# Weight sums of the down projection's sets: another order and other buffers

## The chip, the core and the metric

The kernel runs on one core of a Trainium2 chip. TensorE does the matrix products, VectorE (DVE) and ScalarE (ACT) the elementwise work, GpSimd (POOL) small things, and SyncE (SP) issues most transfers. The metric is the time of one execution on the device in microseconds. Lower is better.

## The reference

The function is two transformer blocks in a row over 256 tokens of width 2048, in float32: a gated-linear-attention mixer and an MLP with a squared ReLU, then a hybrid mixer, a cross attention and a convolutional feed-forward. What matters here is the MLP of the first block, which is

```
def _sq_relu_mlp(h, w_up, w_down):
    a = jax.nn.relu(h @ w_up)          # 2048 -> 8192
    return (a * a) @ w_down            # 8192 -> 2048
```

with a normalised input and its result added to h.

## The kernel before

All weights arrive as a stream of chunks of 128 x 2048 float32 (1 MB). A product in float32 precision is made of three: each operand is split into a high part and a low part, and TensorE adds high x high, high x low and low x high. ScalarE makes the high part of each chunk (`split`, L1198), VectorE subtracts it from the chunk and so makes the low part (`split`, L1874), in place over the raw chunk. The raw chunks go through a ring of four slots, and the high parts through four of their own. A chunk that is used for all 256 tokens takes 24 matmuls of 512 columns (`chunk`, L615 to L617), one that is used for a half of them takes 12 (`product`, L757 to L759).

The MLP works in four parts of 2048 hidden units. A part has up to 38 items, numbered 0 to 37 here: items 0 to 7 are plain up chunks, 8 to 18 a set (`up_pair`), 19 to 26 plain down chunks for the output blocks 0 and 1, and 27 to 37 again a set (`down_pair`), in the first three parts. A set computes blocks 2 and 3 of the output from sums of operands, in the manner of Strassen's algorithm with fewer products: with B11, B12, B21 and B22 for four weight chunks it needs B11+B12, B12+B22, B11+B12+B22 and that plus B21. VectorE forms these in `sums_of_weights`. For the down set the sums are t1, t3, t2 and t4 and stand as items 31, 35, 32 and 36 in TensorE's order; item 29 is B22 itself ("d22"), item 27 is B11 and item 33 is B21. B12 and B22 are fetched aside, right behind the ring's transfer for item 21, and the sum with B12 is then written over it. VectorE also forms sums of the activations, u_raw (`sums_of_a`, c=21 and 22), of which ScalarE makes u_hi and VectorE u_lo (L2147); item 29 is the first that needs them.

Order is fixed by the program. VectorE and ScalarE each run one loop over c = 0 to 37 in a part, and each takes its instructions strictly in that order. In iteration c VectorE does, one after another: `pair_to_h`, `sums_of_weights`, activation work, the add of a finished block to h (blocks 0 and 1 at c=25 and 26, L1950), the subtraction for item c+3, and last `sums_of_a`. ScalarE does u_hi at c=23 ahead of its copy for item 26. TensorE waits for the count `lo_ready` before each item, which the subtraction for that item raises; for item 28 it also waits for block 0's add to h, and for item 29 for u_lo and block 1's. ScalarE's copy for item i waits for the end of item i-4 on TensorE, and for a sum it waits for `sum_ready` to reach the position that the tuple `SUMS` gives. SyncE refills a ring slot when the item that used it is done.

Addresses: a_s is the start of a 48 KB region. The first 8 KB hold `turned` and the next 8 KB `sq` during the squares of the activations, so that a sum may be written over them only when `sq_moved` and `a_low` say that they are done. The 8 KB at a_s + 16 K receive B12.

Of the kernel before, what the change touches and what calls it, by code (L numbers as in the profile page):

```python
# [17 lines left out]
def build(nc, x, x_turned, mem, mem_turned, stream, cols, rows, wglow, wab, wgu, shapes, masks, out):  # L18
# [15 lines left out]
    ACT, ALU, AX = mybir.ActivationFunctionType, mybir.AluOpType, mybir.AxisListType  # L34
# [5 lines left out]
    GROUPS, GROUP = 4, 38  # L40
# [7 lines left out]
    with ExitStack() as ctx:  # L48
# [15 lines left out]
        K = 1024  # L64
# [31 lines left out]
        a_s = take(48 * K)  # L96
# [40 lines left out]
        a_sum = {"T1": a_a + 8 * K, "T3": a_a + 24 * K, "T2": a_s + 16 * K, "T4": a_s + 24 * K}  # L137
        a_sum["b22"] = a_sum["T4"]
        sum_raw = {t: sb(f"raw_{t}", [P, CH], F32, a) for t, a in a_sum.items()}
        sum_lo = {t: sb(f"lo_{t}", [P, CH], F32R, a) for t, a in a_sum.items()}  # L140
        s_raw = sb("s_raw", [P, 4, 4, P], F32, a_s + 32 * K)
        s_lo = sb("s_lo", [P, 4, 4, P], F32R, a_s + 32 * K)
        a_sum.update({"t3": a_s, "t2": a_s + 8 * K, "t1": a_s + 16 * K, "t4": a_s + 24 * K, "d22": a_s + 24 * K})
        for t in ("t1", "t2", "t3", "t4", "d22"):
            sum_raw[t] = sb(f"raw_{t}", [P, CH], F32, a_sum[t])
            sum_lo[t] = sb(f"lo_{t}", [P, CH], F32R, a_sum[t])
# [125 lines left out]
        sum_ready, b12_in, b22_in = sem("sum_ready"), sem("b12_in"), sem("b22_in")  # L272
# [7 lines left out]
        nat_turned, sq_moved, a_high, a_low = [sem(n) for n in ("nat_turned", "sq_moved", "a_high", "a_low")]  # L280
# [76 lines left out]
        def landing(c):  # L357
            return 16 * (c // SLOTS + 1)
# [67 lines left out]
        C_GLA, C_OUT, C_MLP, C_2 = 0, 48, 64, 64 + sum(LENGTH)  # L426
# [1 line left out]
        assert C_FFN + 96 == NITEM  # L428

        SUM_AT = {10: "b22", 12: "T1", 13: "T2", 15: "T3", 16: "T4"}  # L430
        SUMS = (("T1", "T3", "T2", "T4"), ("t3", "t1", "t2", "t4"))
        DOWN_SUM_AT = {29: "d22", 31: "t1", 32: "t2", 35: "t3", 36: "t4"}
        DOWN_AT = {27: (0, 2), 28: (2, 2), 30: (3, 2), 33: (1, 2), 34: (2, 3), 37: (3, 3)}
        UP_AT = {8: (0, 2), 9: (2, 2), 11: (3, 2), 14: (1, 2), 17: (2, 3), 18: (3, 3)}
# [16 lines left out]
        def down_chunk(g, q, b):  # L451
            return C_MLP + 32 * g + 16 + 4 * b + q
# [30 lines left out]
        @block.sync  # L483
        def _(sp):
            x_rows = x.rearrange("(m p) n -> p m n", p=P)

            def quarter_of_x(n):
                sp.dma_start(h[:, :, n * N:(n + 1) * N], x_rows[:, :, n * N:(n + 1) * N]).then_inc(x_in, 16)

            def turned_x(k0, k1, done):  # L490
                sp.dma_start(x_raw[:, k0:k1], x_turned[:, k0:k1]).then_inc(done, 16)

            def weights(c, k):
                sp.dma_start(w_raw[:, c, k * N:(k + 1) * N], stream[c][:, k * N:(k + 1) * N]).then_inc(w_part[c][k], 16)

            turned_x(0, 2, xT_in[0])
            weights(0, 0)
            weights(0, 1)
            turned_x(2, 4, xT_in[NB])
            weights(0, 2)  # L500
            weights(0, 3)
            for c in range(1, EARLY):
                turned_x(4 * c, 4 * c + 4, xT_in[c])
                for k in range(4):
                    weights(c, k)
            sp.dma_start(ident, shapes[:, 0:P]).then_inc(cst_in, 16)
            sp.dma_start(mask01[:], shapes[:, 2 * P:2 * P + SEQ]).then_inc(mask_in, 16)
            for n in range(SLOTS, len(RING)):
                c = RING[n]
                sp.wait_ge(used, RING[n - SLOTS] + 1)  # L510
                sp.dma_start(w_raw[:, n % SLOTS], stream[source(c)]).then_inc(landed[n % SLOTS], 16)
                if C_MLP <= c < C_2 and (c - C_MLP) % GROUP == 3:
                    sp.dma_start(sum_raw["T3"][:], stream[up_chunk((c - C_MLP) // GROUP, 0, 3)]).then_inc(b12_in, 16)
                    sp.dma_start(sum_raw["b22"][:], stream[up_chunk((c - C_MLP) // GROUP, 1, 3)]).then_inc(b22_in, 16)
                if C_MLP <= c < C_MLP + 3 * GROUP and (c - C_MLP) % GROUP == 21:
                    sp.dma_start(sum_raw["t1"][:], stream[down_chunk((c - C_MLP) // GROUP, 0, 3)]).then_inc(b12_in, 16)
                    sp.dma_start(sum_raw["d22"][:], stream[down_chunk((c - C_MLP) // GROUP, 1, 3)]).then_inc(b22_in, 16)
                if c == SLOTS + 1:
                    for n in range(NB):
                        quarter_of_x(n)  # L520
                if c == SLOTS + 4:
                    sp.dma_start(ones, shapes[:, P:2 * P]).then_inc(cst_in, 16)
            for m in range(M):
                sp.wait_ge(fin_dve, 3 * m + 1)
                sp.dma_start(out[m * P:(m + 1) * P, 2 * N:3 * N], h[:, m, 2 * N:3 * N]).then_inc(out_done, 16)
                sp.wait_ge(fin_dve, 3 * m + 3)
                sp.dma_start(out[m * P:(m + 1) * P, 3 * N:4 * N], hlast[:, m]).then_inc(out_done, 16)
            sp.wait_ge(out_done, 16 * 2 * NB)
# [1332 lines left out]
        def _(dve):  # L1861
# [229 lines left out]
            def sums_of_weights(part, c):  # L2091

                first = C_MLP + GROUP * part

                def weights_in(k):
                    dve.wait_ge(landed[PLACE[first + k] % SLOTS], landing(PLACE[first + k]))
                    return raw(first + k)

                if c == 5:
                    b11 = weights_in(8)  # L2100
                    dve.wait_ge(b12_in, 32 * part + 16)
                    dve.tensor_tensor(sum_raw["T1"][:], b11, sum_raw["T3"][:], ALU.add).then_inc(sum_ready, 1)
                if c == 6:
                    dve.wait_ge(b22_in, 32 * part + 16)
                    dve.tensor_tensor(sum_raw["T3"][:], sum_raw["T3"][:], sum_raw["b22"][:], ALU.add).then_inc(sum_ready, 1)
                    dve.wait_ge(sum_ready, 8 * part + 1)
                    dve.tensor_tensor(sum_raw["T2"][:], sum_raw["T1"][:], sum_raw["b22"][:], ALU.add).then_inc(sum_ready, 1)
                if c == 10:
                    b21 = weights_in(14)
                    dve.wait_ge(used, first + 11)  # L2110
                    dve.wait_ge(sum_ready, 8 * part + 3)
                    dve.tensor_tensor(sum_raw["T4"][:], sum_raw["T2"][:], b21, ALU.add).then_inc(sum_ready, 1)
                if part == 3:
                    return
                if c == 23:
                    dve.wait_ge(b12_in, 32 * part + 32)
                    dve.wait_ge(b22_in, 32 * part + 32)
                    dve.wait_ge(sq_moved, 4 * part + 4)
                    dve.tensor_tensor(sum_raw["t3"][:], sum_raw["t1"][:], sum_raw["d22"][:], ALU.add).then_inc(sum_ready, 1)
                if c == 24:  # L2120
                    b11 = weights_in(27)
                    dve.wait_ge(sum_ready, 8 * part + 5)
                    dve.tensor_tensor(sum_raw["t1"][:], sum_raw["t1"][:], b11, ALU.add).then_inc(sum_ready, 1)
                    dve.wait_ge(a_low, 4 * part + 4)
                    dve.tensor_tensor(sum_raw["t2"][:], sum_raw["t3"][:], b11, ALU.add).then_inc(sum_ready, 1)
                if c == 29:
                    b21 = weights_in(33)
                    dve.wait_ge(used, first + 30)
                    dve.wait_ge(sum_ready, 8 * part + 7)
                    dve.tensor_tensor(sum_raw["t4"][:], sum_raw["t2"][:], b21, ALU.add).then_inc(sum_ready, 1)  # L2130

            def sums_of_a(part, c):

                rows_ = [[v_sum[:, q, :, m * P:(m + 1) * P] for q in range(2)] for m in range(M)]
                if c == 21:
                    dve.wait_ge(nat_turned, 4 * part + 4)
                    for q in range(2):
                        ins = dve.tensor_tensor(v_sum[:, q], a_hi[:, 4 * q:4 * q + 4].bitcast(F32), a_lo[:, 4 * q:4 * q + 4].bitcast(F32), ALU.add)
                    link(ins)
                if c == 22:  # L2140
                    dve.tensor_tensor(u_raw[:, 2], rows_[0][0], rows_[1][0], ALU.subtract)
                    link(dve.tensor_tensor(u_raw[:, 0], rows_[1][0], rows_[1][1], ALU.subtract))
                    link(dve.tensor_tensor(u_raw[:, 1], u_raw[:, 0], rows_[0][0], ALU.subtract))
                    dve.tensor_tensor(u_raw[:, 3], u_raw[:, 1], rows_[0][1], ALU.add).then_inc(s_formed, 1)
                if c == 25:
                    dve.wait_ge(pair_out, pair_step(part, "s"))
                    dve.tensor_tensor(u_lo[:], u_raw[:], u_hi[:].bitcast(F32), ALU.subtract).then_inc(s_formed, 1)  # L2147

# [401 lines left out]
            for nb in range(NB):  # L2550
                for j in range(16):
                    c = 50 + 16 * nb + j
# [306 lines left out]
```

## Time and profile before

| | us |
|---|---|
| median of 3 runs | 2473.53 (2472.73 to 2474.16) |
| profiled execution | 2473.63 |
| its span, first to last instruction | 2471.8 |
| TensorE matmuls busy | 2459.8 (100%) |
| VectorE busy | 1660.3 (67%) |
| ScalarE busy | 1608.6 (65%) |

The duration of a matmul in the profile runs past the start of the next one, so "busy" is not the same as "at its peak"; the distance between two starts tells more. The rows used below are from three views. A wait row says who waited for whom, then the total, the number of times and the longest, in us. A timeline row has the start in us from the span's start, the duration, engine, line, operation, tiles and how many instructions were merged, and in brackets the idle time of the engine before it and what ended that. A window row has, for a stretch, the busy time and number of instructions of each engine, the granted TensorE clock (1.00 is 2.4 GHz, 0.50 is 1.2 GHz), the DMA share and the rate in GB/s. Lines are those of the kernel before as the profile numbers them.

### The profile page before, as it was taken

What the parts mean: (1) busy time and instruction counts of PE and PEld (TensorE: products, weight loads), DVE (VectorE), ACT (ScalarE), POOL (GpSimd) and SP (SyncE); (2) the same over time, 40 slices, a digit from 0 to 9 for tenths busy, and PEclk for the clock granted to TensorE, in tenths of its full rate; (3) what the DMA queues carried; (4) which work ended last, traced back from release to release, by engine and by line L of the source; (5) the groups of instructions that cost most, each with busy time, mean ns of one, the idle gap of its engine ahead of it and who ended that gap; (6) DMA issues with size and microseconds to landing.
All of it is one profiled execution on the core that took longest, in us unless ns stands there. A gap on an engine that the chain in (4) does not pass through costs nothing.

```text
span 2471.8 us, 29802 instructions
## 1 busy us (share of the span) xinstructions
PE 2459.8 (100%) x12367; PEld 2030.9 (82%) x12367; DVE 1660.3 (67%) x1371; ACT 1608.6 (65%) x2119; POOL 33.4 (1%) x41
## 2 busy tenths in 40 slices
PE   9999999999999999999999999999999999999998
PEld 7887788888888888888888888888888888888887
DVE  5865658787778868577764785545666677646675
ACT  6545778856748658776465684545586788638873
POOL 0000000000000000000000000000000000000000
PEclk9999999999999999999999999999999999999999
DMA  8554556545554555545443445555655555555554
GB/s 289 187 190 168 173 188 237 190 181 208 206 203 178 215 207 188 189 171 198 158 149 140 157 174 195 196 188 197 261 189 176 192 194 188 199 191 190 200 189 153
DMA packets 69366, 472.36 MB, mean 191 GB/s; under 512 B 7912, under 2 KB 8352, under 8 KB 13424
## 3 DMA queue, kind: packets, MB, share of 16 engines
q1 hardware_dynamic: 67040, 460.62, 51.5%
q0 software_dynamic: 1312, 7.73, 0.8%
q8 instruction: 97, 1.59, 0.3%
q10 hardware_dynamic: 880, 2.11, 0.2%
q14 instruction: 37, 0.30, 0.0%
HBM read 468.33 MB, written 2.11 MB: 190 GB/s over the span
## 4 chain that ended last, share of the span: by engine, by line
PE 93%; DVE 2%; ACT 2%; issue 1%; DMA 1%; SPq 0%; POOLq 0%; POOL 0%; DVEq 0%; ACTq 0%
PE acc L615 28%; PE acc L617 28%; PE acc L616 28%; DMA w_raw<-in_stream 1%; PE tp L759 1%; PE tp L758 1%; PE tp L757 1%; ACT w_hi L1198 1%; DVE w_lo L1874 1%; PE acc L757 1%; PE acc L759 1%; PE acc L758 1%; ACT sq L1391 1%; PE tp L979 1%; PE tp L912 0%
## 5 line engine op out<-in xcount | busy, mean ns | idle before, releaser
L1874 DVE TENSOR_TENSOR w_lo<-w_raw,w_hi 128x2048 fp32r<-128x2048 f32 x416 | 950.9, 2288 | 616.4 <-ACT w_hi L1198 614.2
L1198 ACT ACTIVATE w_hi<-w_raw 128x2048 fp32r<-128x2048 f32 x416 | 795.6, 1915 | 394.3 <-DMA w_raw<-in_stream 346.8
L615 PE MATMUL acc<-w_hi,x_hi 128*128 128x512 f32 (+1 forms) x2112 | 826.2, 391 | 1.4 <-DVE w_lo L1881 0.6
L617 PE MATMUL acc<-w_hi,x_lo 128*128 128x512 f32 (+1 forms) x2112 | 819.7, 388 | 0.0
L616 PE MATMUL acc<-w_lo,x_hi 128*128 128x512 f32 (+1 forms) x2112 | 819.5, 388 | 0.0
L615 PEld LDWEIGHTS acc<-w_hi,x_hi 128*128 128x128 f32 x2112 | 396.8, 188 | 86.8 <-issue 2.9
L617 PEld LDWEIGHTS acc<-w_hi,x_lo 128*128 128x128 f32 x2112 | 396.7, 188 | 81.3
L616 PEld LDWEIGHTS acc<-w_lo,x_hi 128*128 128x128 f32 x2112 | 396.9, 188 | 80.3 <-issue 1.0
L615 PE MATMUL acc<-w_hi,a_hi 128*128 128x512 f32 x1024 | 400.0, 391 | 0.4 <-DVE w_lo L1874 0.2
L616 PE MATMUL acc<-w_lo,a_hi 128*128 128x512 f32 x1024 | 399.0, 390 | 0.0
L617 PE MATMUL acc<-w_hi,a_lo 128*128 128x512 f32 x1024 | 398.9, 390 | 0.0
L615 PEld LDWEIGHTS acc<-w_hi,a_hi 128*128 128x128 f32 x1024 | 192.3, 188 | 42.4 <-DVE w_lo L1874 1.6
L617 PEld LDWEIGHTS acc<-w_hi,a_lo 128*128 128x128 f32 x1024 | 192.3, 188 | 39.7
L616 PEld LDWEIGHTS acc<-w_lo,a_hi 128*128 128x128 f32 x1024 | 192.3, 188 | 39.5
L1391 ACT ACTIVATE sq<-turned 32x256 f32<-32x256 f32 x256 | 106.2, 415 | 6.9 <-DVE turned L2204 3.4
L1788 ACT ACTIVATE fm<-fturned 32x256 f32<-32x256 f32 x256 | 106.2, 415 | 4.5 <-DVE fturned L2689 1.5
L1215 ACT ACTIVATE nat<-acc,rstd 128x512 f32<-128x512 f32 (+1 forms) x80 | 50.0, 677 | 76.4 <-PE acc L617 75.2
L1215 ACT ACTIVATE nat<-acc,rhalf 128x512 f32<-128x512 f32 x36 | 22.8, 684 | 66.8 <-PE acc L617 66.7
L1950 DVE TENSOR_TENSOR h<-acc,h 128x1024 f32<-128x1024 f32 x35 | 42.7, 1221 | 27.4 <-PE acc L617 27.4
L1237 ACT ACTIVATE sq<-turned 32x256 f32<-32x256 f32 x112 | 46.5, 415 | 9.4 <-DVE turned L1917 8.1
L615 PE MATMUL acc<-w_hi,m_hi 128*128 128x512 f32 x128 | 49.9, 390 | 0.0
L616 PE MATMUL acc<-w_lo,m_hi 128*128 128x512 f32 x128 | 49.9, 389 | 0.0
(482 smaller groups left out, 1954.2 us busy)
## 6 DMA issues: line engine op xcount, KB each, us to landing
w_raw<-in_stream SPq DMA_DIRECT2D x416, 1024.0 KB, 4.8
w_raw<-in_stream SPq DMA_DIRECT2D x16, 256.0 KB, 8.2
raw_T<-in_stream SPq DMA_DIRECT2D x4, 1024.0 KB, 7.2
raw_b<-in_stream SPq DMA_DIRECT2D x4, 1024.0 KB, 8.9
raw_t<-in_stream SPq DMA_DIRECT2D x3, 1024.0 KB, 7.0
raw_d<-in_stream SPq DMA_DIRECT2D x3, 1024.0 KB, 10.2
h<-in_x SPq DMA_DIRECT2D x4, 512.0 KB, 14.0
frow<-in_rows POOLq DMA_DIRECT2D x2, 1024.0 KB, 6.5
```

What stands on the lines that cost most here:

```text
L615: pe.matmul(dst, xh, wh[:, k], start=first and k == 0, stop=False)
L616: pe.matmul(dst, xh, wl[:, k], start=False, stop=False)
L617: mm = pe.matmul(dst, xl, wh[:, k], start=False, stop=last and k == n_k - 1)
L757: pe.matmul(dst, xh[:, k], wh[:, k], start=start and k == 0, stop=False, skip_group_check=not start)
L758: pe.matmul(dst, xh[:, k], wl[:, k], start=False, stop=False, skip_group_check=not start)
L759: mm = pe.matmul(dst, xl[:, k], wh[:, k], start=False, stop=stop and k == 3, skip_group_check=not start)
L1198: act.activation(w_hi[:, c % SLOTS], raw(c), ACT.Copy).then_inc(hi_ready, 1)
L1215: ins = act.activation(dst[:, m], src[:, m], func, scale=scales[:, j, m:m + 1])
L1237: ins = act.activation(dst[32 * to:32 * to + 32, :, :, q], src[32 * q:32 * q + 32, :, :, to], ACT.Copy, scale=scale)
L1391: ins = act.activation(dst[32 * to:32 * to + 32, :, :, q], src[32 * q:32 * q + 32, :, :, to], ACT.Square)
L1788: ins = act.activation(dst[32 * to:32 * to + 32, :, :, q], src[32 * q:32 * q + 32, :, :, to], ACT.Copy)
L1874: dve.tensor_tensor(low_part(c), raw(c), w_hi[:, c % SLOTS].bitcast(F32), ALU.subtract).then_inc(lo_ready, 1)
```

## The change

The four sums of a down set are formed in the order t1, t3, t2, t4, and not t3, t1, t2, t4. B12 is fetched into the buffer t3, which has the address that t1 had, so it lands in the same place; t1 has the address that t3 had. t1 = B11 + B12 stays at c=24, now as the first sum. t3 = B12 + B22 goes from c=23 to c=25, in place over B12. t2 goes from c=24 to c=26 and is computed as t1 + B22, not as t3 + B11. The subtraction u_lo goes from c=25 to c=24. The waits go with the sums. TensorE's program is the same.

```
-        a_sum.update({"t3": a_s, "t2": a_s + 8 * K, "t1": a_s + 16 * K, "t4": a_s + 24 * K, "d22": a_s + 24 * K})
+        a_sum.update({"t1": a_s, "t2": a_s + 8 * K, "t3": a_s + 16 * K, "t4": a_s + 24 * K, "d22": a_s + 24 * K})
...
-        SUMS = (("T1", "T3", "T2", "T4"), ("t3", "t1", "t2", "t4"))
+        SUMS = (("T1", "T3", "T2", "T4"), ("t1", "t3", "t2", "t4"))
...
-                    sp.dma_start(sum_raw["t1"][:], stream[down_chunk((c - C_MLP) // GROUP, 0, 3)]).then_inc(b12_in, 16)
+                    sp.dma_start(sum_raw["t3"][:], stream[down_chunk((c - C_MLP) // GROUP, 0, 3)]).then_inc(b12_in, 16)
...
-                if c == 23:
-                    dve.wait_ge(b12_in, 32 * part + 32)
-                    dve.wait_ge(b22_in, 32 * part + 32)
-                    dve.wait_ge(sq_moved, 4 * part + 4)
-                    dve.tensor_tensor(sum_raw["t3"][:], sum_raw["t1"][:], sum_raw["d22"][:], ALU.add).then_inc(sum_ready, 1)
                 if c == 24:
                     b11 = weights_in(27)
+                    dve.wait_ge(b12_in, 32 * part + 32)
+                    dve.wait_ge(sq_moved, 4 * part + 4)
+                    dve.tensor_tensor(sum_raw["t1"][:], b11, sum_raw["t3"][:], ALU.add).then_inc(sum_ready, 1)
+                if c == 25:
+                    dve.wait_ge(b22_in, 32 * part + 32)
+                    dve.tensor_tensor(sum_raw["t3"][:], sum_raw["t3"][:], sum_raw["d22"][:], ALU.add).then_inc(sum_ready, 1)
+                if c == 26:
+                    dve.wait_ge(a_low, 4 * part + 4)
                     dve.wait_ge(sum_ready, 8 * part + 5)
-                    dve.tensor_tensor(sum_raw["t1"][:], sum_raw["t1"][:], b11, ALU.add).then_inc(sum_ready, 1)
-                    dve.wait_ge(a_low, 4 * part + 4)
-                    dve.tensor_tensor(sum_raw["t2"][:], sum_raw["t3"][:], b11, ALU.add).then_inc(sum_ready, 1)
+                    dve.tensor_tensor(sum_raw["t2"][:], sum_raw["t1"][:], sum_raw["d22"][:], ALU.add).then_inc(sum_ready, 1)
...
-                if c == 25:
+                if c == 24:
                     dve.wait_ge(pair_out, pair_step(part, "s"))
                     dve.tensor_tensor(u_lo[:], u_raw[:], u_hi[:].bitcast(F32), ALU.subtract).then_inc(s_formed, 1)
```

## Rows read from the trace of the kernel before

**Rows 1.** The page's head and its first part: busy us, share, instructions.
```profile
span 2471.8 us, 29802 instructions
...
PE 2459.8 (100%) x12367; PEld 2030.9 (82%) x12367; DVE 1660.3 (67%) x1371; ACT 1608.6 (65%) x2119; POOL 33.4 (1%) x41
```

**Rows 2.** The list of waits, TensorE: total us, times, longest.
```profile
PE acc L615 <- DVE w_lo L1874: 0.5, 2, 0.3
```

**Rows 3.** Timeline of TensorE, first part: first matmuls of items 27, 28, 29, 32.
```profile
508.62 0.39 PE L757 MATMUL tp<-w_hi,a_hi 128*128 128x512 f32 x1
...
511.12 0.39 PE L759 MATMUL tp<-w_hi,a_lo 128*128 128x512 f32 x1
511.62 0.50 PE L615 MATMUL acc<-w_hi,a_hi 128*128 128x512 f32 x1
...
517.25 0.47 PE L757 MATMUL acc<-w_hi,u_hi 128*128 128x512 f32 x1
...
528.23 0.39 PE L757 MATMUL tp<-w_hi,u_hi 128*128 128x512 f32 x1
```

**Rows 4.** Timeline of VectorE, first part.
```profile
495.47 2.29 DVE L2119 TENSOR_TENSOR raw_t<-raw_t,raw_d 128x2048 f32<-128x2048 f32 x1
499.34 2.29 DVE L1874 TENSOR_TENSOR w_lo<-w_raw,w_hi 128x2048 fp32r<-128x2048 f32 x1 [1.58 <-ACT w_hi L1198]
501.55 2.28 DVE L2123 TENSOR_TENSOR raw_t<-raw_t,w_raw 128x2048 f32<-128x2048 f32 x1
...
505.95 2.28 DVE L1874 TENSOR_TENSOR w_lo<-w_raw,w_hi 128x2048 fp32r<-128x2048 f32 x1
...
509.29 2.28 DVE L1874 TENSOR_TENSOR w_lo<-w_raw,w_hi 128x2048 fp32r<-128x2048 f32 x1
511.49 2.28 DVE L2147 TENSOR_TENSOR u_lo<-u_raw,u_hi 128x2048 fp32r<-128x2048 f32 x1
...
514.82 2.28 DVE L1874 TENSOR_TENSOR lo_d<-raw_d,w_hi 128x2048 fp32r<-128x2048 f32 x1
...
524.22 2.29 DVE L1874 TENSOR_TENSOR lo_t<-raw_t,w_hi 128x2048 fp32r<-128x2048 f32 x1
...
541.32 2.29 DVE L1874 TENSOR_TENSOR w_lo<-w_raw,w_hi 128x2048 fp32r<-128x2048 f32 x1 [1.94 <-ACT w_hi L1198]
```

**Rows 5.** Timelines of VectorE and TensorE, item 28 of second and third part.
```profile
678.41 2.28 DVE L1874 TENSOR_TENSOR w_lo<-w_raw,w_hi 128x2048 fp32r<-128x2048 f32 x1
...
680.74 0.50 PE L615 MATMUL acc<-w_hi,a_hi 128*128 128x512 f32 x1
...
847.72 2.28 DVE L1874 TENSOR_TENSOR w_lo<-w_raw,w_hi 128x2048 fp32r<-128x2048 f32 x1
...
850.05 0.51 PE L615 MATMUL acc<-w_hi,a_hi 128*128 128x512 f32 x1 [0.18 <-DVE w_lo L1874]
```

**Rows 6.** Timeline of ScalarE, first part: u_hi and the copies of 26 and 27.
```profile
495.58 1.92 ACT L1451 ACTIVATE u_hi<-u_raw 128x2048 fp32r<-128x2048 f32 x1 [5.01 <-DVE u_raw L2144]
497.41 3.70 ACT L1198 ACTIVATE w_hi<-w_raw 128x2048 fp32r<-128x2048 f32 x2
```

**Rows 7.** Timeline of TensorE, a longer gap near the kernel's start.
```profile
13.45 0.50 PE L615 MATMUL acc<-w_hi,x_hi 128*128 128x512 f32 x1 [0.64 <-DVE w_lo L1881]
13.78 0.39 PE L616 MATMUL acc<-w_lo,x_hi 128*128 128x512 f32 x1
```

**Rows 8.** TensorE's last matmul, and windows behind it (PEclk is third from the end).
```profile
2463.55 0.39 PE L617 MATMUL acc<-w_hi,a_lo 128*128 128x512 f32 x1
...
2465.00:2466.00 1.00, 0.00 (x0) 0.00 (x0) 0.56 (x2) 0.43 (x2) 0.30 (x1) 1.00 0.00 0
2466.00:2467.00 1.00, 0.00 (x0) 0.00 (x0) 0.71 (x2) 0.65 (x1) 0.25 (x1) 0.73 0.00 0
```

**Rows 9.** Timeline of TensorE's weight loads, the kernel's first matmuls.
```profile
1.59 0.15 PEld L728 LDWEIGHTS acc<-junk 128*128 128x128 bf16 x1 [0.28 <-issue]
...
5.43 0.33 PEld L728 LDWEIGHTS acc<-junk 128*128 128x128 bf16 x2 [0.28 <-issue]
```

## The prediction

> **What bounds the kernel now.** The page's first part comes first: TensorE is busy for 2459.8 of 2471.8 us [rows 1]. Whatever the change does to VectorE counts only where it moves a matmul. The list of waits then names few for TensorE; the one that belongs to a subtraction of a weight chunk (L1874) sums to 0.5 us [rows 2]. That list understates it, because the end of a matmul is modelled: one start every 0.227 us (508.62 to 511.12 is 11 intervals) but 0.39 us of duration, so a short stall is covered by the record before it. So I read starts in the timeline. Around the start of chunk 28 of the first part two starts are 0.50 us apart, 511.12 and 511.62 [rows 3], 0.27 more than the steady interval. From 511.12 to 528.23 there are 73 intervals (24 of chunk 28, 12 of 29, 24 of 30, 12 of 31, and one), 16.6 us at 0.227; they took 17.11. About 0.55 us are lost there per part.
>
> What releases chunk 28 is seen on VectorE. Its subtraction for chunk 28 runs 509.29 to 511.57 and TensorE starts 0.05 later [rows 3, 4]. The other two parts show the same pair: subtraction 678.41 to 680.69, matmul 680.74; subtraction 847.72 to 850.00, matmul 850.05 [rows 5]. Three out of three times the end of this one subtraction sets the start of chunk 28, and TensorE has no slack there.
>
> VectorE is late because it works without a pause from 499.34 (subtraction for 26) until the 1.94 us before 541.32; no row between those two has idle time in its brackets [rows 4]. Before 499.34 it has a hole of another sort: the subtraction for 26 waits 1.58 us for ScalarE's copy of 26, which stands behind the copy u_hi (495.58), so it can't be done before 499.3 [rows 6]. VectorE reaches that point at 495.47, and the first sum of the set (L2119) lies wholly in this gap: 495.47 to 497.76 [rows 4]. It costs nothing now.
>
> **The change part by part.** Per part with a down set (three of four) VectorE has the same four sums and the same u_lo; no instruction is added or removed, and none changes its length. What counts is the order between the subtraction for 26 and that for 28.
>
> *Before:* sub 26, t1, t2, sub 27, add to h, sub 28; then u_lo, add to h, sub 29, sub 30.
> *After:* sub 26, t1, sub 27, u_lo, t3, add to h, sub 28; then t2, add to h, sub 29, sub 30.
>
> The end of c=23 loses the sum L2119: the gap before 499.34 grows from 1.58 to about 3.9 us, and nothing is gained, since the subtraction for 26 is released by ScalarE, whose two copies don't depend on the sum [rows 4, 6]. Removed: 0.
>
> c=24: t1 stays in place. t2 goes (a 2048-element operation; start to start 2.20 us, as 499.34 to 501.55 and 509.29 to 511.49 show [rows 4]). So the subtraction for 27 starts at 503.75 and not at 505.95. It ended at 508.24, with chunk 27 starting at 508.62 [rows 3, 4]: TensorE didn't wait for it, so 2.20 us earlier is worth 0. Then u_lo, 2.20, takes the place that is freed. Its input u_hi is done by 497.5 [rows 6], so it doesn't wait.
>
> c=25: the sum t3, another 2.20 us, now stands ahead of the add to h and of the subtraction for 28. Its transfers came with item 21, long before; the sums of before took the same two buffers at 495.47 without a wait [rows 4]. Nothing lets VectorE do it while idle.
>
> Sum for the subtraction for 28: −t2 + u_lo + t3 = −2.20 + 2.20 + 2.20 = +2.20 us. It starts at 511.49, ends at 513.77, and chunk 28 starts at about 513.82 in place of 511.62. Queued behind t3 on VectorE are the add to h of block 0 and subtraction 28, and TensorE waits for the second. The bounds on a 2048-element operation are 2.20 (start to start) and 2.28 to 2.29 (its full duration, if nothing overlaps). I take 2.20, since all rows in an unbroken run show it.
>
> Chunk 29: before, u_lo, the add and the subtraction for 29 followed (subtraction start 509.29 to 514.82 is 5.53 us). After, t2 is where u_lo was, equally long: again 5.53. Chunk 29 therefore keeps its present small delay, and u_lo, which it also needs, is earlier. Its subtraction starts at 517.02. Of the later ones, the subtraction for 32 starts at 524.22 and chunk 32's products at 528.23, 1.7 us after it ends [rows 3, 4]. Both sides move by 2.20, and so does ScalarE, which waits for the counts of finished chunks. t2 is ready at 515.97, ahead of ScalarE's copy of it, which waits for the end of chunk 28 at about 519.3. The fourth sum L2130 reads t2, and waits for chunk 29 as before. The 1.94 us of idle before 541.32 belongs to a wait for ScalarE that itself follows TensorE, so it pays nothing back: work follows matmuls there, and every matmul is late by 2.20.
>
> A larger stall could also have a larger ramp behind it. After 511.62 the intervals are a little long (0.34, then 0.24), part of the 0.55. At the start of the kernel a longer gap, with 0.64 us of recorded idle, ends at 13.45, and the next start follows 0.33 later [rows 7]; the ramp doesn't grow with the gap. I add 0, bound +0.15 per part. From below: the existing 0.55 per part could vanish if the order mattered in a way that I don't see, 1.65 in all.
>
> DMA: the transfer of the fourth chunk has another name, but t3 now has the address that t1 had, and its place on SP's queue stays. Cost 0. The waits on counts a_low, sum_ready and sq_moved are for events that VectorE has itself passed, or that lie before 495. Cost 0.
>
> Sum: 3 × 2.20 = 6.6 us on the profiled execution's 2473.63, which is its span 2471.8 and 1.8 around it: 2480.2. The median shown is 2473.53, 0.1 lower, so this is +0.27%.
>
> The Trainium skill ("VectorE: DVE Perf Modes", section "The DRAIN you can't avoid") has the next VectorE operation start only when the pipeline is empty. The rows of an unbroken run show a start 0.08 us ahead of the recorded end of the one before. By the rule's word an extra operation would be 2.28 and the sum 6.8 us, 2480.4; the rows decide for 2.20.
>
> **The rivals.** *The clock falls in the longer gap.* In the changed kernel TensorE would have no matmul from 511.51 to 513.82, 2.3 us, three times. At the end of the kernel the last matmul ends at 2463.94, the granted clock is 1.00 to 2466 and averages 0.73 over the next microsecond: with the two levels 2.4 and 1.2 GHz it fell at about 2466.5, after 2.5 us without a matmul [rows 8]. That is near. Against it: the gap here is shorter and has dense matmuls on both sides. What a fall would cost: in the kernel's first matmuls the loads are 0.43 us apart from 1.59 to 5.43 [rows 9], nearly twice 0.227; some 4.2 us at that pace lose 2.0 us. One to three falls give 2482.2 to 2486.2.
> The Trainium skill ("TensorE: Matmul & The Clock Gate", section "Why this matters for your kernels") warns of gaps between bursts, since idle time brings the clock down, but allows longer ones than 2.3 us; by it the sum is left at 2480.2. The row at the end of the kernel shows a fall after less idle time than it allows, so I keep the rival.
>
> *Not slower.* The wider hole at c=23 pays the operation back. With the sum gone from beside ScalarE's copies, the copy of 26 would end sooner, VectorE would begin its unbroken run earlier, and the extra operation would be done before it is missed. It decides from a subtraction for 26 that starts 2.2 us earlier, near 497.1; then nothing changes, 2473.6, and if it starts another 0.5 earlier the present loss goes too: 2472.0. For it: VectorE is ready at 495.5, so only ScalarE holds the start. Against: the copy of 26 starts at 497.41, since u_hi before it starts only at 495.58, released by u_raw, which the change doesn't touch [rows 6]; and the two copies take 3.70 us together with the sum running beside only the first moments of them.
>
> *A second wait of the same size.* One operation more is late at chunk 29 or 32 too, because a copy or sum that I count as covered isn't. One more 2.20 per part gives 2486.8. Against it: the 5.53 us that stays and the 1.7 us of slack at 32.
>
> **How the numbers follow.** Forecast 0.76, own range 2479.0 to 2481.5; clock 0.10; not slower 0.08; second wait 0.06. The range 2477.6 to 2484.0 leaves out the not-slower case, the second wait and half of the clock's, 0.19. Told apart from no change is 0.2%, 4.9 us, so slower begins at 2478.5: forecast, clock and second wait less 0.04 for a forecast that comes out small, 0.88. Within: 0.08 less 0.01, and those 0.04: 0.11. Faster 0.01, since all that can be won in this stretch is 1.65 us.
>
> **What would show it.** In the timeline of the changed kernel: a hole of 3.9 us on VectorE before the subtraction for 26; the order after it as above; subtraction 28 ending 14.4 us after the start of subtraction 26 (12.2 now); gaps of 2.7 us between matmul starts at chunk 28, three of them; the waits list with some 2.3 us each for TensorE on L1874; chunk 29 with the small delay of now; the clock 1.00 throughout. The forecast is wrong if chunk 28 starts before subtraction 28 ends, if the subtraction for 26 starts earlier than now relative to chunk 26, or if matmul intervals near 0.43 us follow the gap.

## The result and the profile after

The changed kernel takes 2482.12 us (median of 6 runs, 2481.78 to 2484.38), the kernel before 2473.79 (6 runs): ratio 1.0036, interval 1.0025 to 1.0048. It is slower by 8.3 us. The profiled execution took 2484.38, the longest of the six, with a span of 2482.6. One execution of a later kernel (the one with matmuls in the gap) took 4771.94 us at a mean granted clock of 0.512 and stands in no ratio here.

The head of the page of the changed kernel and its wait of TensorE on L1874, which answer to [rows 1, 2]:

```profile
span 2482.6 us, 29802 instructions
...
PE 2462.9 (99%) x12367; PEld 2032.3 (82%) x12367; DVE 1660.5 (67%) x1371; ACT 1609.0 (65%) x2119; POOL 33.5 (1%) x41
```
```profile
PE acc L615 <- DVE w_lo L1874: 7.9, 4, 2.7
```

The number of instructions and VectorE's and ScalarE's busy time are as before. What changed is waiting: TensorE's wait for this subtraction, 0.5 us in all, became 7.9. VectorE's timeline of the changed kernel, first part, answers to [rows 4] and to the hole of [rows 6]:

```profile
499.83 2.29 DVE L1874 TENSOR_TENSOR w_lo<-w_raw,w_hi 128x2048 fp32r<-128x2048 f32 x1 [3.79 <-ACT w_hi L1198]
502.04 2.28 DVE L2119 TENSOR_TENSOR raw_t<-w_raw,raw_t 128x2048 f32<-128x2048 f32 x1
504.25 2.28 DVE L1874 TENSOR_TENSOR w_lo<-w_raw,w_hi 128x2048 fp32r<-128x2048 f32 x1
506.45 2.28 DVE L2148 TENSOR_TENSOR u_lo<-u_raw,u_hi 128x2048 fp32r<-128x2048 f32 x1
508.65 2.28 DVE L2122 TENSOR_TENSOR raw_t<-raw_t,raw_d 128x2048 f32<-128x2048 f32 x1
510.85 1.21 DVE L1950 TENSOR_TENSOR h<-acc,h 128x1024 f32<-128x1024 f32 x1
511.99 2.28 DVE L1874 TENSOR_TENSOR w_lo<-w_raw,w_hi 128x2048 fp32r<-128x2048 f32 x1
```

The hole before the subtraction for 26 is 3.79 us where it was 1.58, and from the start of that subtraction to the end of the one for 28 it is 14.44 us (511.99 + 2.28 − 499.83) where it was 12.23. The extra 2.2 are t3 (L2122). TensorE in the same stretch, and further down its gaps in parts two and three, answer to [rows 3, 5]:

```profile
511.31 0.39 PE L759 MATMUL tp<-w_hi,a_lo 128*128 128x512 f32 x1
514.32 0.50 PE L615 MATMUL acc<-w_hi,a_hi 128*128 128x512 f32 x1 [2.62 <-DVE w_lo L1874]
514.66 0.55 PE L616 MATMUL acc<-w_lo,a_hi 128*128 128x512 f32 x1
515.01 0.63 PE L617 MATMUL acc<-w_hi,a_lo 128*128 128x512 f32 x1
515.43 0.63 PE L615 MATMUL acc<-w_hi,a_hi 128*128 128x512 f32 x1
515.86 0.63 PE L616 MATMUL acc<-w_lo,a_hi 128*128 128x512 f32 x1
...
518.30 0.39 PE L616 MATMUL acc<-w_lo,a_hi 128*128 128x512 f32 x1
518.53 0.39 PE L617 MATMUL acc<-w_hi,a_lo 128*128 128x512 f32 x1
...
687.54 0.50 PE L615 MATMUL acc<-w_hi,a_hi 128*128 128x512 f32 x1 [2.68 <-DVE w_lo L1874]
...
860.48 0.50 PE L615 MATMUL acc<-w_hi,a_hi 128*128 128x512 f32 x1 [2.35 <-DVE w_lo L1874]
```

Two things are to be seen. Item 28 starts 0.05 us after its subtraction ends, as before, and 3.01 us after the start of the last matmul of item 27. And the matmuls behind the gap start 0.43 us apart from 515.01 to 518, then 0.23 again. Windows of the changed kernel (the granted clock stands third from the end):

```profile
511.30:514.30 3.00, 0.40 (x2) 0.00 (x0) 3.00 (x3) 1.91 (x1) 0.00 (x0) 1.00 0.98 391
514.30:514.90 0.60, 0.58 (x2) 0.54 (x3) 0.60 (x1) 0.00 (x0) 0.00 (x0) 0.87 1.00 423
515.00:518.20 3.20, 3.20 (x9) 2.51 (x8) 3.20 (x3) 0.00 (x0) 0.00 (x0) 0.51 0.25 102
518.30:520.00 1.70, 1.70 (x9) 1.39 (x8) 1.70 (x2) 0.00 (x0) 0.00 (x0) 1.00 0.00 0
...
688.60:689.00 0.40, 0.40 (x3) 0.35 (x2) 0.40 (x1) 0.00 (x0) 0.00 (x0) 0.77 0.97 389
...
860.50:866.00 5.50, 5.50 (x24) 4.40 (x24) 5.50 (x4) 0.00 (x0) 0.00 (x0) 1.00 0.32 137
```

The clock, 2.4 GHz through the gap, went to 1.2 GHz shortly after it (0.87 is the mean of the first 0.6 us), when matmuls ran again, and came back at about 518.3. It did the same in the second part, where it fell at about 688.8 (the row that starts at 688.60), and not in the third (the last row).

The account of the profiled execution, +10.75 us: the gaps between matmul starts at item 28 were 0.50, 0.42 and 0.56 and are 3.01, 3.06 and 2.74, 7.3 more. From the start of item 28 to that of item 30 TensorE took 8.45, 8.47 and 8.45 us before and takes 9.90, 9.95 and 8.44 now: 1.45 and 1.48 more in the two parts with a fall and 0 in the third, 2.9 in all. The other 0.5 us lie outside what was changed: 0.2 were there before the first of these gaps (the last matmul of item 27 starts at 511.31, not 511.12), and 0.35 came in behind item 30 of the third part (from 858.50 to the last matmul at 2463.55 before, from 868.92 to 2474.32 now). Their cause is open.

### The profile page after: what moved, and what is told of

Its sections match the earlier page's. It is cut to its first block, busy times and chain, and to the rows that moved or that the text cites. A ratio compares the mean times of both kernels' runs of the same rounds, so it can differ in the third digit from the quotient of the medians.

```text
span 2482.6 us, 29802 instructions
## 1 busy us (share of the span) xinstructions
PE 2462.9 (99%) x12367; PEld 2032.3 (82%) x12367; DVE 1660.5 (67%) x1371; ACT 1609.0 (65%) x2119; POOL 33.5 (1%) x41
## 4 chain that ended last, share of the span: by engine, by line
PE 91%; DVE 3%; ACT 2%; issue 2%; DMA 1%; SPq 0%; POOLq 0%; POOL 0%; DVEq 0%; ACTq 0%
PE acc L615 28%; PE acc L617 27%; PE acc L616 27%; DMA w_raw<-in_stream 1%; ACT w_hi L1198 1%; DVE w_lo L1874 1%; PE tp L759 1%; PE tp L758 1%; PE tp L757 1%; PE acc L757 1%; PE acc L758 1%; PE acc L759 1%; ACT sq L1391 1%; PE tp L979 1%; PE tp L912 0%
## 5 line engine op out<-in xcount | busy, mean ns | idle before, releaser
L1874 DVE TENSOR_TENSOR w_lo<-w_raw,w_hi 128x2048 fp32r<-128x2048 f32 x416 | 950.8, 2288 | 625.4 <-ACT w_hi L1198 622.8
L617 PE MATMUL acc<-w_hi,m_lo 128*128 128x512 f32 x128 | 49.8, 389 | 0.0
```

The lines of the kernel that those rows point to most:

```text
L617: mm = pe.matmul(dst, xl, wh[:, k], start=False, stop=last and k == n_k - 1)
L1874: dve.tensor_tensor(low_part(c), raw(c), w_hi[:, c % SLOTS].bitcast(F32), ALU.subtract).then_inc(lo_ready, 1)
```

## The experiments

Three theories went in. A: one more operation in VectorE's unbroken run is the cost, 2.2 us a part, and the clock's falls follow from the gap. B: the new buffers, the in-place sum or the later t2 cost something themselves. C: only the late t3 matters, wherever u_lo stands. The 1.7 us that B has to explain are what the measured 8.3 has beyond the forecast's 6.6. Each kernel was run 5 to 11 times beside the kernel before, whose median was 2473.31 for the first four and 2473.88 for the rest.

**u_lo back at c=25.**

```
-                if c == 24:
+                if c == 25:
                     dve.wait_ge(pair_out, pair_step(part, "s"))
```

> The changed kernel with u_lo back at c=25, behind the subtraction for 28; the sums stay in their new order and buffers. Theory A (what counts is how many operations stand between the subtraction for 26 and that for 28, and the clock falls in the gap that one more of them makes): the count is that of the kernel before again, so no long gap, clock 0.999, 2473.8 within 0.7 us. Rival B (new buffers, in-place sum or later t2 cost something of their own, the 1.7 us beyond 6.6): 2475.5. Rival C (u_lo's place is of no account, the late sum t3 is what costs): 2482.

Measured: 2481.59 us, ratio 1.0033 (1.0021 to 1.0046). A's number, 2473.8, was wrong. The trace shows where its counting stopped too early. TensorE of this kernel:

```profile
516.69 0.39 PE L617 MATMUL acc<-w_hi,a_lo 128*128 128x512 f32 x1
519.16 0.47 PE L757 MATMUL acc<-w_hi,u_hi 128*128 128x512 f32 x1 [2.09 <-DVE lo_d L1874]
```

Up to the subtraction for 28 the count is indeed that of before. But between those for 28 and 29 now stand both u_lo and t2, where before only u_lo stood. The gap moved to item 29: 2.47, 2.50 and 2.44 us in the three parts, with one fall of the clock in the profile, behind the first, where the stretch from the start of item 29 to that of item 31 took 9.88 us against 8.25 and 8.28 in the other two. An operation that has left the hole is in the run somewhere; where u_lo stands decides only which item pays. This run alone speaks for C, whose 2482 it nearly is, and A stands only in this wider form. For the total the wider A and C then say the same, but for one point: whether it must be t3 that is late. The next run answers that.

**One more operation in the kernel before.**

```
...
-                    dve.tensor_tensor(sum_raw["t2"][:], sum_raw["t3"][:], b11, ALU.add).then_inc(sum_ready, 1)
+                    dve.tensor_tensor(sum_raw["t2"][:], sum_raw["t3"][:], b11, ALU.add).then_inc(formed_once, 1)
+                if c == 25:
+                    dve.wait_ge(sum_ready, 8 * part + 6)
+                    dve.wait_ge(formed_once, 1 * part + 1)
+                    dve.tensor_tensor(sum_raw["t2"][:, :2048], sum_raw["t1"][:, :2048], sum_raw["d22"][:, :2048], ALU.add).then_inc(sum_ready, 1)
```

> The kernel before with one more VectorE operation of 2048 elements ahead of the subtraction for 28: t2 is formed a second time at c=25. Order and buffers of the sums are those of before. A: one operation is 2.2 us in each of three parts, 6.6, and one to three falls of the clock at 1.6 us each, so 2482 to 2485, like the changed kernel. B: 2480.4, since nothing but the operation is added and the rest came with the buffers. C: 2480 to 2482 as well.

Measured: 2482.13 us, ratio 1.0035 (1.0023 to 1.0047), the changed kernel's time, with buffers and order of before. B is out as the cause of the 1.7 us beyond 6.6, and t3 need not be the one that is late: here it stands in the hole. In the profile of this kernel (its lines are numbered one higher) the gap and the first slow intervals of the first part, and the two ends of the third part's gap and fall:

```profile
511.33 0.39 PE L760 MATMUL tp<-w_hi,a_lo 128*128 128x512 f32 x1
513.93 0.50 PE L616 MATMUL acc<-w_hi,a_hi 128*128 128x512 f32 x1 [2.21 <-DVE w_lo L1875]
514.27 0.42 PE L617 MATMUL acc<-w_lo,a_hi 128*128 128x512 f32 x1
514.50 0.62 PE L618 MATMUL acc<-w_hi,a_lo 128*128 128x512 f32 x1
514.92 0.63 PE L616 MATMUL acc<-w_hi,a_hi 128*128 128x512 f32 x1
...
857.77 0.50 PE L616 MATMUL acc<-w_hi,a_hi 128*128 128x512 f32 x1 [1.90 <-DVE w_lo L1875]
...
859.26 0.63 PE L616 MATMUL acc<-w_hi,a_hi 128*128 128x512 f32 x1
```

The gaps between starts were 2.60, 2.65 and 2.29 us, and the clock fell behind the first and the third: the shortest took a fall and the longest did not.

**Matmuls in the gap of the changed kernel**, nine behind item 27.

```
...
+                for k in range(fill):
+                    mm = pe.matmul(tpf(0)[:, N:2 * N], xh[:, k % 4], wh[:, k % 4], start=True, stop=True)
                 mm.then_inc(used, 1)
...
-                product(c0 + 27, *of_a(0, 0), chain, start=True, stop=True)
+                product(c0 + 27, *of_a(0, 0), chain, start=True, stop=True, fill=9)
```

> The changed kernel with nine more matmuls of 512 columns behind item 27 (2.04 us at 0.227), operands of item 27, written to the half bank that item 31 later starts anew, so that TensorE works while it would wait for the subtraction for 28. A: the stall stays, so chunk 28 starts no earlier, but the clock stays at 1.00: 2480.2 to 2480.9, the clock's part (1.7 us in the median of the changed kernel) gone. B: no change, 2482.

Measured: 2479.82 us over all eight executions, 2479.68 over the seven that the ratio takes, 1.0026 (1.0016 to 1.0037). That is 27 matmuls more and 2.8 us less than the changed kernel on the same chip (2482.46, the next run). Above the kernel before it is 6.4 us, against 6.6 in the forecast. TensorE of this kernel, first part, and its clock behind:

```profile
510.90 2.20 PE L761 MATMUL tp<-w_hi,a_hi 128*128 128x512 f32 x9
513.33 0.50 PE L615 MATMUL acc<-w_hi,a_hi 128*128 128x512 f32 x1 [0.23 <-DVE w_lo L1876]
513.67 0.39 PE L616 MATMUL acc<-w_lo,a_hi 128*128 128x512 f32 x1
```
```profile
513.40:518.00 4.60, 4.60 (x20) 3.79 (x21) 4.60 (x3) 1.72 (x1) 0.00 (x0) 1.00 0.61 228
```

Item 28 still waits for its subtraction. Only the idle time is gone, and with it the slow intervals, in all three parts.

**The changed kernel again.**

> The changed kernel again, on the same chip. A: 2481.8 to 2484.4, with one or two of the three gaps followed by about 3.4 us at the lower clock, each gap 2.7 to 3.1 us between matmul starts, and which parts they are may differ from the first profile. B: the same time with the clock at 1.00 in one profile or the other.

Measured: 2482.46 us (2480.32 to 2482.81), ratio 1.0036 (1.0023 to 1.0048). In this profile the clock fell in the first and the third part and not in the second:

```profile
685.70:690.00 4.30, 4.30 (x19) 3.57 (x20) 4.30 (x3) 0.00 (x0) 0.00 (x0) 1.00 0.42 177
...
857.60:861.00 3.40, 3.40 (x10) 2.67 (x9) 3.40 (x3) 0.00 (x0) 0.00 (x0) 0.54 0.37 154
512.90:516.40 3.50, 3.50 (x9) 2.75 (x10) 3.50 (x3) 0.00 (x0) 0.00 (x0) 0.53 0.47 197
```

Its gaps were 2.76, 2.68 and 2.65, so of the last two the shorter took a fall and the longer did not. Four of the five executions had a mean clock of 0.998 and took 2482.2 to 2482.8; the fifth, at 0.999 like the kernel before, took 2480.32.

**t3 back in the hole, the rest of the change kept.**

```
+                if c == 23:
+                    dve.wait_ge(b12_in, 32 * part + 32)
+                    dve.wait_ge(b22_in, 32 * part + 32)
+                    dve.wait_ge(sq_moved, 4 * part + 4)
+                    dve.tensor_tensor(sum_raw["t3"][:], sum_raw["t1"][:], sum_raw["d22"][:], ALU.add).then_inc(sum_ready, 1)
...
-                if c == 25:
-                    dve.wait_ge(b22_in, 32 * part + 32)
-                    dve.tensor_tensor(sum_raw["t3"][:], sum_raw["t3"][:], sum_raw["d22"][:], ALU.add).then_inc(sum_ready, 1)
```

t1 and t3 have the buffers and the order of before with it.

> The change with one part of it undone: the sum t3 is back at c=23, in VectorE's gap ahead of the subtraction for 26 (and so t3 and t1 keep the buffers and the order of before); t2 = t1 + B22 at c=26 and u_lo at c=24 stay as changed. A (the operation that left the gap is the whole cost, 2.2 us a part, and the clock follows from it): the operations between the subtractions for 26, 28 and 29 are as many as before, so 2473.3 within 0.7 us, gaps of 0.4 to 0.6 us at item 28, clock 0.999. B (the later t2 or the earlier u_lo costs): between 2475 and 2482.

Measured: 2473.77 us, ratio 1.0 (0.9991 to 1.0008). The whole loss is undone; u_lo at c=24 and t2 from t1 at c=26 cost nothing that can be measured. In its profile the gaps at item 28 were 0.45, 0.62 and 0.71 us, the last two somewhat longer than the 0.4 to 0.6 expected, with no slow interval behind them. As the buffers went back together with t3, this run alone doesn't part the two; the kernel with one more operation did, which had the buffers of before and the full loss.

**t1 in the hole as well**, in the kernel before.

```
...
-                if c == 24:
                     b11 = weights_in(27)
                     dve.wait_ge(sum_ready, 8 * part + 5)
                     dve.tensor_tensor(sum_raw["t1"][:], sum_raw["t1"][:], b11, ALU.add).then_inc(sum_ready, 1)
+                if c == 26:
                     dve.wait_ge(a_low, 4 * part + 4)
-                    dve.tensor_tensor(sum_raw["t2"][:], sum_raw["t3"][:], b11, ALU.add).then_inc(sum_ready, 1)
+                    dve.wait_ge(sum_ready, 8 * part + 6)
+                    dve.tensor_tensor(sum_raw["t2"][:], sum_raw["t1"][:], sum_raw["d22"][:], ALU.add).then_inc(sum_ready, 1)
```

> The kernel before with t1 at c=23 too, ahead of the subtraction for 26, and t2 = t1 + B22 at c=26. A: VectorE's unbroken run begins with t3 at 495.5 and goes on with t1 at 497.7, the subtraction for 26 starts some 0.5 us later than now (its item starts at 503.2, so that is hidden) and the one for 28 ends 3 to 4 us earlier than now; the 1.7 us of stalls in the three parts go, 2471.7, a gain near what can be told apart. B: the chunk for item 27 lands after 497.7 and t1's wait for it holds the subtraction for 26, so 2473.3 or more.

Measured: 2472.08 us, ratio 0.9993 (0.9984 to 1.0002): 1.8 us less in the medians, but the interval holds 1, so the times alone don't show a gain. The trace shows that the small stalls are gone. VectorE of this kernel:

```profile
495.02 2.28 DVE L2119 TENSOR_TENSOR raw_t<-raw_t,raw_d 128x2048 f32<-128x2048 f32 x1
497.41 2.29 DVE L2122 TENSOR_TENSOR raw_t<-raw_t,w_raw 128x2048 f32<-128x2048 f32 x1
499.62 4.49 DVE L1874 TENSOR_TENSOR w_lo<-w_raw,w_hi 128x2048 fp32r<-128x2048 f32 x2
504.02 1.22 DVE L1950 TENSOR_TENSOR h<-acc,h 128x1024 f32<-128x1024 f32 x1
505.15 2.29 DVE L1874 TENSOR_TENSOR w_lo<-w_raw,w_hi 128x2048 fp32r<-128x2048 f32 x1
```

Two sums lie ahead of the subtraction for 26, which starts some 0.7 us later than it could, since ScalarE's copies of 26 and 27 begin at 496.96 and the subtraction followed 1.93 us behind that start in the kernel before [rows 4, 6]; its item starts only at 502.7. The subtraction for 28 ends at 507.44, 3.5 us before its item starts, and from 480 to 960 us no two matmul starts that the timeline lists are over 0.23 us apart, where the kernel before has 0.50, 0.42 and 0.56 at item 28. From the first matmul of item 27 in the first part to the kernel's last, TensorE takes 1953.30 us (508.18 to 2461.48) where it took 1954.93 (508.62 to 2463.55): 1.6 less. Its median is the lowest of the kernels run here.

**Half an operation more, and two more**, each in the kernel before at c=25.

```
...
+                    dve.tensor_tensor(sum_raw["t2"][:, :1024], sum_raw["t2"][:, :1024], sum_raw["t2"][:, :1024], ALU.max).then_inc(sum_ready, 1)
```
```
...
+                    dve.tensor_tensor(sum_raw["t2"][:, :2048], sum_raw["t1"][:, :2048], sum_raw["d22"][:, :2048], ALU.add).then_inc(formed_once, 1)
+                    dve.wait_ge(formed_once, 2 * part + 2)
+                    dve.tensor_tensor(sum_raw["t2"][:, :2048], sum_raw["t1"][:, :2048], sum_raw["d22"][:, :2048], ALU.add).then_inc(sum_ready, 1)
```

> The kernel before with one more VectorE operation of 1024 elements (1.13 us) at c=25, ahead of the subtraction for 28: half of t2 is overwritten with itself. A: 3 x 1.13 = 3.4 us, and the gap between matmul starts is 1.6 us, after which the clock stays at 1.00: 2476.7. If the clock falls after so short a gap as well: 2478.3 or more. B (cost doesn't follow the operation's length): 2473.3 or 2480.

> The kernel before with two more VectorE operations of 2048 elements ahead of the subtraction for 28 (t2 formed twice more at c=25). A: 6 x 2.2 = 13.2 us, gaps of 4.9 us, and the clock falls in each of the three: 3 x 1.6 = 4.8 us or somewhat less where it falls inside the gap, 2489.5 to 2491.5. If the clock follows a gap only by chance of its phase, however long the gap is, with one fall or none: 2486.5 to 2488.

Measured: half, 2477.10 us, ratio 1.0014 (1.0005 to 1.0022), 3.2 more than before against 3.4 expected; its gaps were 1.78, 1.56 and 1.66 us with no slow interval after them. Its first part, with a full pace again 0.33 us behind the gap:

```profile
512.70 0.50 PE L616 MATMUL acc<-w_hi,a_hi 128*128 128x512 f32 x1 [1.39 <-DVE w_lo L1875]
513.03 0.40 PE L617 MATMUL acc<-w_lo,a_hi 128*128 128x512 f32 x1
513.27 0.39 PE L618 MATMUL acc<-w_hi,a_lo 128*128 128x512 f32 x1
```

Two more: 2493.09, ratio 1.0079 (1.0066 to 1.0093), 19.2 more, above the 2489.5 to 2491.5 that A gave. Of those, 13.2 are operations and 6 are the clock, not the 4.8 expected. The trace agrees: from item 28 to item 30 this kernel took 10.71, 9.82 and 10.99 us against 8.45, 8.47 and 8.45, so the falls cost 2.3, 1.4 and 2.5. Its gaps were 4.96, 5.04 and 4.96 us. The first part:

```profile
513.40:514.40 1.00, 0.00 (x0) 0.00 (x0) 1.00 (x1) 0.00 (x0) 0.00 (x0) 0.65 0.98 418
514.40:515.30 0.90, 0.00 (x0) 0.00 (x0) 0.90 (x2) 0.00 (x0) 0.00 (x0) 0.50 0.53 219
515.40:520.50 5.10, 5.10 (x12) 4.04 (x13) 5.10 (x3) 0.00 (x0) 0.00 (x0) 0.50 0.00 0
520.70:522.00 1.30, 1.30 (x8) 1.04 (x7) 1.30 (x2) 0.00 (x0) 0.00 (x0) 1.00 0.00 0
```

Here the clock fell inside the gap, at about 513.7, 2.9 us after the last matmul's recorded end, and the matmuls ran at 1.2 GHz for 5 us after it. In the other two parts it held longer, some 4.5 and 3.5 us behind that end (the granted clock was 0.96 from 690.00 to 691.30 and 0.61 from 865.00 to 866.30), and the slow stretches after the gap were 3 and 5.6 us. So three gaps of nearly one length cost different amounts.

## Why the prediction was right, and where not

*What bounds.* Right. Reading starts and not idle times found the 0.5 us gaps, and the subtraction for 28 as their cause; its end set item 28 to within 0.06 us in all three parts of the changed kernel too (511.99 + 2.28 and 514.32, 685.21 + 2.28 and 687.54, 858.14 + 2.28 and 860.48).

*The count of operations.* Right. The removal from c=23 widened the hole to 3.8 us and gained nothing; the subtraction for 28 came 2.2 us later after that for 26; an operation in the run took 2.21 us from start to start (502.04 to 504.25), the forecast's 2.20; 28 to 29 stayed 5.53 us (511.99 to 517.52). The kernel with t3 alone put back is as fast as before, the one with the gap filled costs 6.4 us, 0.2 under the forecast's sum. The rival that the wider hole pays it back is out: counted from item 27, the subtraction for 26 started at most 0.03 us earlier, not 2.2. So is the second wait of the same size: from the first gap to 960 us the changed kernel's only starts over 0.43 us apart are the three at item 28.

*The clock: the step that failed.* I gave its fall 0.10 and left it out of the predicted time, "Against it: the gap here is shorter and has dense matmuls on both sides". It fell in two of three gaps in both profiles, and every execution of the changed kernel but one of eleven took 2481.78 or more, above the forecast's own range. The rival's time for one fall, 2482.2, is the measured median within 0.1, but that is luck. Both profiles of the changed kernel had two falls, 2.9 us together, and the profiled execution of 2482.22 reached item 27 of the first part 1.1 us earlier than the kernel before did in its profile (507.54 against 508.62), ahead of anything changed. The price of 2.0 us a fall was somewhat high: eight intervals of 0.43 in place of 0.227 are 1.6, and 1.4 to 1.5 net of the ramp that they replace. It came from the pace at the kernel's start, a stretch for which the profile records a clock of 1.00; that 0.43 is the pace at 1.2 GHz is shown only by the runs here. Right in the profile was the 0.73 row behind the last matmul [rows 8]; wrong was to set the shorter gap and a rule on a page against it. The Trainium skill ("TensorE: Matmul & The Clock Gate", section "Why this matters for your kernels") allows longer idle gaps than any of these, and the traces don't agree: of the six gaps in the two profiles of the changed kernel, with 2.26 to 2.68 us of recorded idle time, four were followed by a fall, and so was one with 1.90 in the kernel with one more operation.

*The gap's length.* Forecast 2.70 us between starts, measured 3.01, 3.06 and 2.74. The subtraction for 26 started 0.30, 0.44 and −0.03 us later than before, counted from the last matmul of item 27. In the first part this goes back to a copy on ScalarE at 473.97 that waited for a transfer, 473.47 before, ahead of anything changed. The repeat had 2.76, 2.68 and 2.65. So it is a matter of single executions.

*Range and chances.* The range held the time, slower was given 0.88. The right number came from the range's reach to the rival, not from the likeliest case.

What stays open: which of three like gaps takes the fall, and when. It was parts one and two in one profile of the changed kernel and one and three in the other. The length of the gap doesn't decide it in this range: in the four profiles of the changed kernel (two), of u_lo back and of one more operation, 7 of 12 gaps of 2.29 to 3.06 us took a fall, that of 2.29 among them, while one of 2.74 did not.

## What to carry to other kernels

An engine that is not the bound can still have a stretch without slack; there, count its operations between two signals that the bounding engine waits for, and look for holes upstream: an operation in a hole is free, and the same operation 13 us later costs its full length. Where such a stall grew to between 2.3 and 3.1 us between two matmul starts, the clock fell in 7 of 12 cases here, so its price belongs in the sum: 1.7 to 2.8 us on 6.6. Count every pair of signals behind the edit, not only the first, or the stall just moves on to the next item.

## What the runs showed of the hardware

The clock can fall after a gap as well as in it. With gaps of 2.3 to 3.1 us between starts it stayed at 2.4 GHz through the gap, and where it fell it went to 1.2 only after matmuls had resumed: 1.3 us after in the changed kernel's second part (687.54 to 688.8), 1.5 in the third part of the kernel with one more operation (857.77 to 859.26). Gaps of 1.6 to 1.8 us showed no slow intervals in the profile taken. Those of 5.0 us did in all three parts, and there the fall came 2.9, 4.5 and 3.5 us after the last matmul's recorded end. Nine matmuls whose result nobody reads, put into each gap, made the kernel 2.8 us faster than the same kernel without them. A float32 operation of 2048 elements on VectorE is recorded with 2.28 us, and the next one in the run starts 2.20 after it.
